# Hybrid decoder step on one core: eight of fourteen input-projection panels per layer computed by seven block products on token halves

## What is computed

```
def mixing_block(x, st, l, P, lb, pos0):
    ...
    proj = jnp.einsum('btd,de->bte', x, P['w_in'][l]).astype(jnp.float32)
    ...
    (xa, ga, qb, kb, vb, ob, ib, fb, qc, kc, vc, gc, qd, fd, id_, gd) = jnp.split(proj, cuts, axis=-1)
    ...
    ya, h1, buf1 = rglru_group(xa, ga, ...)
    yb, c1, n1, m1 = mlstm_group(qb, kb, vb, ob, ib, fb, ...)
    yc, sr1 = retention_group(qc, kc, vc, gc, ...)
    yd, sh1 = hgrn2_group(qd, fd, id_, gd, ...)
    mixed = jnp.concatenate([ya, yb, yc, yd], axis=-1).astype(x.dtype)
```

## Time and profile before

| | |
|---|---|
| time, median of 3 runs | 1056.05 us (1053.13 to 1056.63) |
| the profiled execution's own time | 1044.64 us |
| its span | 1042.8 us |
| input projection and mixers, layer one | about 8 to 180.4 us |
| output projection and normalization, layer one | 180.4 to 217 us |
| dense feed-forward | 217 to 455 us |
| layer two's mixers | the same chain, 447 us later |
| experts and end | 675 to 1042.8 us |

### The profile page before, as it was taken

The page is one execution under the profiler, slowest core; times in us unless marked ns, Lnnn a source line. Parts: engine busy times, 40 slices in busy tenths (PEclk is TensorE's granted clock), DMA queues, the critical chain, the costliest instruction groups (busy, mean ns, idle before and its releaser), DMA issues.

```text
span 1042.8 us, 22726 instructions
## 1 busy us (share of the span) xinstructions
PE 1023.0 (98%) x10341; PEld 740.8 (71%) x10341; DVE 434.4 (42%) x853; ACT 181.8 (17%) x393; POOL 94.3 (9%) x102
## 2 busy tenths in 40 slices
PE   9999999999999999999999999999999999999995
PEld 6787776899999999987877768744545545455552
DVE  5654725555656664148447352621101012010225
ACT  1322223041111100043232231500000000000011
POOL 2000123700000000000011210041000020000010
PEclk9999999999999999999999999999999999999998
DMA  9452238504454235104521429699999999999963
GB/s 334 151 202 82 69 118 301 220 1 162 162 192 162 82 126 228 67 19 143 203 79 44 145 88 367 252 325 357 422 407 409 416 402 408 425 421 424 424 262 113
DMA packets 36548, 240.17 MB, mean 230 GB/s; under 512 B 4768, under 2 KB 8096, under 8 KB 16736
## 3 DMA queue, kind: packets, MB, share of 16 engines
q1 hardware_dynamic: 26896, 216.40, 53.0%
q0 software_dynamic: 6416, 19.52, 5.4%
q10 hardware_dynamic: 3136, 2.75, 0.8%
HBM read 228.60 MB, written 13.07 MB: 232 GB/s over the span
## 4 chain that ended last, share of the span: by engine, by line
PE 93%; DVE 4%; ACT 1%; DMA 1%; issue 1%; SPq 0%; DVEq 0%
PE ps L669 72%; PE ps L1169 14%; PE ps L1274 5%; PE ps L672 1%; DMA up_slots<-in_w_in 1%; DVE x L1992 1%; DVE overlay L1987 0%; ACT overlay L1598 0%; DVE overlay L2123 0%; DVE up_slots L2094 0%; DVE mix_or_moe L2121 0%; DVE overlay L2122 0%; ACT L1598 0%; ACT up_slots L1598 0%; DVE tables L2660 0%
## 5 line engine op out<-in xcount | busy, mean ns | idle before, releaser
L669 PE MATMUL ps<-up_slots,mix_or_moe 128*32 128x352 f32 (+2 forms) x3248 | 245.3, 451 | 0.0
L669 PE MATMUL ps<-x,up_slots 128*128 128x288 f32 (+2 forms) x944 | 233.2, 399 | 0.8 <-DMA up_slots<-in_w_in 0.8
L669 PEld LDWEIGHTS ps<-x,up_slots 128*128 128x128 f32 x944 | 168.9, 190 | 50.8 <-issue 8.3
L669 PEld LDWEIGHTS ps<-up_slots,mix_or_moe 128*32 128x32 f32 (+2 forms) x3248 | 106.6, 111 | 130.5 <-issue 128.8
L669 PE MATMUL ps<-overlay,tables 128*32 128x256 f32 (+5 forms) x2020 | 125.6, 375 | 0.3 <-DVE overlay L1981 0.2
L669 PEld LDWEIGHTS ps<-overlay,tables 128*32 128x32 f32 (+2 forms) x2020 | 76.6, 114 | 46.9 <-issue 5.3
L1169 PE MATMUL ps<-overlay,up_slots 128*128 128x144 f32 x704 | 91.2, 286 | 1.2 <-DVE overlay L2479 1.2
L1169 PEld LDWEIGHTS ps<-overlay,up_slots 128*128 128x128 f32 x704 | 88.2, 190 | 1.4 <-issue 1.4
L669 PE MATMUL ps<-overlay,up_slots 128*128 128x128 f32 (+3 forms) x560 | 86.0, 314 | 1.0 <-ACT overlay L1598 1.0
L2699 DVE TENSOR_TENSOR mix_or_moe<-mix_or_moe,ps 128x352 f32<-128x352 f32 x24 | 11.2, 517 | 178.3 <-PE ps L669 178.3
L669 PEld LDWEIGHTS ps<-overlay,up_slots 128*128 128x128 f32 x560 | 78.2, 191 | 8.6 <-ACT overlay L1598 1.9
(11 more groups left out here) (329 smaller groups left out, 901.2 us busy)
## 6 DMA issues: line engine op xcount, KB each, us to landing
up_slots<-in_moe_w SPq DMA_DIRECT2D x64, 1408.0 KB, 21.0
overlay<-in_moe_w SPq DMA_DIRECT2D x21, 1536.0 KB, 22.5
up_slots<-in_ffn_w SPq DMA_DIRECT2D x30, 1024.0 KB, 6.9
up_slots<-in_w_in SPq DMA_DIRECT2D x27, 1024.0 KB, 4.9
up_slots<-in_w_out SPq DMA_DIRECT2D x8, 1024.0 KB, 9.3
overlay<-in_moe_w SPq DMA_DIRECT2D x7, 1024.0 KB, 22.4
mix_or_moe<-in_states POOLq DMA_DIRECT2D x6, 512.0 KB, 10.5
out_sample_states<-mix_or_moe POOLq DMA_DIRECT2D x6, 512.0 KB, 6.0
```

Of the source, the lines that this page charges most:

```text
L669: return pe.matmul(o, lhsT, rhs, start=start, stop=stop)
```

## The change

Panels 5 to 12 of each layer (VB, KC, QC, ID, VC, GA, GD, GC) are computed by block products. A panel's weights W are four blocks (two halves of the 1024 input channels by its two tiles of outputs), X is four blocks (two halves of the channels by two halves of 144 tokens). Seven products of one weight block or sum of blocks with one X block or sum of blocks take the place of eight; each is four matmuls of 128x128 on 144 tokens. For these panels:

- DVE makes four sums of X once per layer (`token_sums`, 576 elements each), four sums of weights per panel (`panel_sums`, 512 each), and from the products the two output tiles (`panel_outputs`, five operations of 144 and one of 288).
- PE computes the products in three groups of 2, 3 and 2, each group side by side in one PSUM bank, the banks alternating.
- ACT copies each group to SBUF (288, 432 and 288 elements), and before that waits until DVE has used up the same group of the panel before.
- SP loads a panel's blocks once PE has done all products of the panel two before; the output projection's first three weight panels are loaded at the end of the stage and no longer in its middle, the fourth as before after the mLSTM's sample states.
- A tile of such a panel counts as ready when DVE's `panel_outputs` has ended (before: when ACT's copy had).
- On ACT the square and deviation of the retention's norm stand earlier in the order. On the host the weights of these panels are stored block by block.

```
+SEVEN = range(5, 13)
+SEVEN_GROUPS = ((0, 2), (2, 5), (5, 7))
...
+                def token_sums():
...
+                    v.wait_ge(S["in_ps"], N_IN * l + 8)
+                    b11, b12, b21, b22 = (X[:, k:k + KH, c] for k in (0, KH) for c in TOKEN_HALVES)
+                    sig(tt(TX[:, 0], b11, b12, SU), S["sx_t"], 4 * l + 1)
+                    sig(tt(TX[:, 1], b22, TX[:, 0], AD), S["sx_t"], 4 * l + 2)
+                    tt(TX[:, 2], b12, b22, SU).then_inc(S["sx_t"], 1)
+                    tt(TX[:, 3], TX[:, 1], b21, SU).then_inc(S["sx_t"], 1)
...
+                def panel_sums(q, steps=(0, 1, 2, 3)):
+                    w11, w12, w22, w21, s2, s4, s1 = BLOCKS[q % 2]
+                    if 0 in steps:
+                        v.wait_ge(S[f"sx_in_{q % 2}"], loaded["seven", l, q])
+                        tt(s1, w21, w22, AD).then_inc(S["sx_w"], 1)
+                        v.wait_ge(*seven_sum(l, q, 0))
+                    if 1 in steps:
+                        tt(s2, s1, w11, AD).then_inc(S["sx_w"], 1)
+                    if 2 in steps:
+                        tt(w21, w21, w11, AD).then_inc(S["sx_w"], 1)
+                    if 3 in steps:
+                        v.wait_ge(*seven_sum(l, q, 1))
+                        tt(s4, s2, w12, AD).then_inc(S["sx_w"], 1)
...
+                def first_outputs(q):
...
+                    v.wait_ge(*seven_group("sx_ac", l, q, 1))
+                    tt(proj[:, tile, 0:TH], p1, p2, AD)
+                    sig(tt(p6, p6, p1, SU), *seven_out(l, q, 0))
...
+                def last_outputs(q):
...
+                    v.wait_ge(*seven_group("sx_ac", l, q, 2))
+                    tt(p3, p3, p5, AD)
+                    link(tt(p7, p7, p6, AD))
+                    tt(proj[:, tile, TH:T], p3, p6, SU)
+                    sig(tt(proj[:, tile + 1].rearrange("p (h t) -> p h t", h=2), p7.unsqueeze(1).to_broadcast([P, 2, TH]),
+                           SEVEN_OUT[1][:, 0:2], SU), *seven_out(l, q, 1))
...
                 merge(6, 2)
                 chunk_ends()
+                panel_sums(4, (0, 1))
                 mlstm_states()
+                panel_sums(4, (2, 3))
                 merge(7, 2)
...
                 mlstm_spread()
+                panel_outputs(4)
                 need("hg_ps", "c0")
...
+                panel_sums(6)
                 head_rstd(RR_ML, SD_ML, "ml_dv")
...
+                def seven(q, g):
+                    act.wait_ge(*seven_group("sx_pe", l, q, g))
+                    if N_SEVEN * l + q:
+                        act.wait_ge(*seven_out(l, q - 1, min(g, 1)))
...
+                    f(SEVEN_OUT[g], PS[:, (3 * q + g) % 2, 0:n * TH].rearrange("p (n t) -> p n t", n=n), ACT.Copy
+                      ).then_inc(S["sx_ac"], 1)
```

More of the change, by code:

```diff
@@ L209, in mark, with dense, seven_group, seven_sum @@
             return S[name], len(STEPS[name]) * l + STEPS[name].index(step) + 1
+        def dense(i):
+            return i if i // 2 < SEVEN.start else i - 2 * N_SEVEN
+        def seven_group(name, l, q, g):
+            return S[name], 3 * (N_SEVEN * l + q) + g + 1
+        def seven_sum(l, q, i):
+            return S["sx_w"], 4 * (N_SEVEN * l + q) + i + 1
+        def seven_out(l, q, i):
+            return S["sx_dv"], 2 * (N_SEVEN * l + q) + i + 1
         def ev(tile, l):
-            return S["in_ev"], N_IN * l + 2 * ORDER.index(tile - tile % 2) + tile % 2 + 1
+            panel = ORDER.index(tile - tile % 2)
+            if panel in SEVEN:
+                return seven_out(l, panel - SEVEN.start, 1)
+            return S["in_ev"], N_IN * l + dense(2 * panel + tile % 2) + 1
         def ffn(name, step, n):
@@ L342, in decoder_kernel @@
         WD = [cut(UPF, 2048 * s[0], 2 * KD, 256) for s in DOWN_SLOTS]
+        TX = cut(UPF, 3584, 4, KH, TH)
+        BLOCKS = [[cut(UPF, at + 512 * j, KH, P) for j in range(7)] for at in SEVEN_AT]
+        SEVEN_OUT = [cut(UPF, at, n, TH) for at, n in ((9472, 2), (9760, 3), (6 * 2048 + 9530, 2))]
         def panels(name):
@@ L433, in _, with seven_in @@
                     sp.wait_ge(S["up_ps"], 11)
-                for i, tile in enumerate(ORDER):
+                def seven_in(q):
+                    b = q % 2
+                    loaded["seven", l, q] = loaded.get(("n seven", b), 0) + 16
+                    loaded["n seven", b] = loaded["seven", l, q]
+                    sp.dma_start(UPF[:, SEVEN_AT[b]:SEVEN_AT[b] + 2048], w_in[l][SEVEN.start + q]).then_inc(S[f"sx_in_{b}"], 16)
+                for i in range(SEVEN.start):
                     if i >= 2:
@@ L1714, in mix @@
                 level(6)
-                tile(14)
+                seven(2, 0)
                 need("lru_dv", "decay")
@@ L2820, in _arrays @@
     w = a["w_in"]
-    arrays["w_in"] = _panels(w, [128 * tile + (8 if tile >= QC else 0) for tile in ORDER])
+    panels = _panels(w, [128 * tile + (8 if tile >= QC else 0) for tile in ORDER])
+    blocks = panels[:, SEVEN.start:SEVEN.stop].reshape(DEPTH, N_SEVEN, P, 2, KH, 2, P)
+    order = [blocks[:, :, :, half, :, out] for out, half in ((0, 0), (0, 1), (1, 1), (1, 0))]
+    panels[:, SEVEN.start:SEVEN.stop] = np.stack(order, 3).reshape(DEPTH, N_SEVEN, P, -1)
+    arrays["w_in"] = panels
     gates = np.zeros((DEPTH, P, KT, HR), np.float32)
```

199 lines of the change are left out of this document (136 added, 63 removed).

## The result

The changed kernel takes **1064.17 us** (median of 5 runs, 1062.3 to 1066.14) against 1053.13 us for the kernel before (5 runs, 1052.06 to 1056.63): ratio **1.0094, 95% interval 1.007 to 1.0118**. It is slower by some 11 us. I had forecast 1054.9 us, 1046 to 1062, with 0.33 for slower: the time is 2 us outside the range and on the other side of no change. (The forecast stood on a median of 1056.05 us for the kernel before; as a ratio it is 0.9989.)

What follows compares the result with a forecast made beforehand. PE, busy for 98% of the span, was taken to bound the kernel. Per layer, -7.7 us saved plus waits of 1.0, 1.3 and 4.8 gave -0.6, -1.2 in all: 1056.05 to 1054.9 us, range 1046 to 1062.

Steps and rivals of the forecast that it cites:

- 0.33 for slower: Chance of a slower kernel: POOL met twice (0.20), DVE or weights late (0.11), narrow matmuls at their mean cost (0.02).
- PE's saving: Eight changed panels a layer, 28 narrow matmuls for 16 wide: 7.7 us a layer, 15.4 us in all.
- DVE's work: New token sums, weight sums and outputs on DVE: 40 us a layer, some 80 us busy time in all.
- Place 1: Sample states of the mLSTM: PE waits 1.0 us a layer for DVE's states.
- Place 2: The panel VC, behind the retention's scores: PE waits 1.3 us a layer for DVE's outputs of VC.
- Place 3: The mLSTM's head scale: PE waits 4.8 us a layer for DVE's reciprocal, delayed by POOL's third product.
- the instruction named: At the mLSTM's head scale, one weight sum of the seventh changed panel lasts 3 us or more beside POOL.
- POOL's second product: Rival: it starts before DVE's scaled sample queries and holds them, +1.9 us a layer, 1059.9 us; chance 0.20.
- the sum: Per layer PE's saving of 7.7 us less waits of 1.0, 1.3 and 4.8: -0.6 us, -1.2 in all.
- the output projection's second panel: Its weights, issued when the last tile ends, cost PE 0, with bounds of 0 to 1.5 us a layer.
- kind: Prediction is wrong in kind if PE waits for transfers, or for ACT, by more than a microsecond a layer.
- the first one I had named: Sign over the whole kernel: PE's busy time falls by about 15 us, its idle time grows by about 14.

Runs made afterwards that it cites:

- r13: Kernel before with the matmuls of tiles 10 to 25 split into two token halves of 144, nothing left out: ratio 1.0001.
- r10: Kernel before with the fourth of eight matmuls left out of each wide tile 10 to 25, outputs incomplete: ratio 0.9865.
- r7: Changed kernel with the reciprocal ahead of the seventh panel's sums, some fifth- and sixth-panel sums later, clearing later, two feed-forward loads earlier: ratio 1.0092.
- r2: Changed kernel with nine filler matmuls of 288 columns, result unused, ahead of PE's wait for the mLSTM's reciprocal: ratio 1.0052.
- r11: Kernel before with the mLSTM's reciprocal computed four times over, giving PE a wait there: ratio 1.018.
- r3: Changed kernel with POOL's eight clearing transfers of the expert tokens moved behind its feed-forward weight sums: ratio 1.0064.
- r4: The changed kernel again, as it is, against the kernel before on one chip: ratio 1.0103.
- r6: Changed kernel with every weight sum of the changed panels working on one column of 128, so the sums are not computed: ratio 0.9947.
- r9: Changed kernel with c1's copy and reciprocal before the seventh panel's sums, POOL's second and third products later, r7's fifth- and sixth-panel sums, r3's clearing: ratio 0.9885.
- r1: Changed kernel with POOL's third product of each layer waiting until DVE's reciprocal for the mLSTM is done: ratio 0.999.
- r12: As r10, one of eight steps left out of tiles 10 to 25, but each matmul of 288 as two of 144: ratio 0.9867.
- r0: The kernel before again, no edit, run for its profile: ratio 1.0003.
- r5: Changed kernel with DVE taking the mLSTM's reciprocal ahead of the seventh changed panel's weight sums: ratio 1.0105.
- r8: Changed kernel with both r1's edit and r3's edit: ratio 0.9932.

## Why the prediction was wrong

**What held.** PE's saving: 0.245 us a narrow matmul, shown alone by r13 (1.0001), and 15.4 us by count; r10, which leaves out 15.6 us of wide matmuls, is 14 faster with 2.0 us of waits of its own. DVE's work: 80 forecast, 80.4 found. Place 1: 1.0 forecast, 0.96 found. Place 2: 1.3 and 0.92. Place 3: 4.8 and 4.40, by the instruction named. POOL's product there began within DVE's third weight sum and lasted 3.90 instead of 3.62 us, so DVE held it up by a little, too, as the prediction allowed. POOL's second product was not met, as the sum assumed, but that is luck: my own numbers put POOL (119.95) ahead of the queries (120.0), and it came out the other way by 0.15 us. r7 shows the price of the other side.

**What failed** is the step called the sum, in the sentence that behind place 3 "PE waits for nothing new by my count", and in what the sum has no term for. An idle microsecond of PE was priced at one microsecond.

1. **The granted clock behind a wait** was left at 0. It is 10.0 us in the profiled execution, found by its windows, shown by r2 (no idle time, no half clock behind it) and r11 (the wait alone brings it).
2. **Layer one's norm** was left at 0. POOL's weight sums for the feed-forward are late, and the fold of squares meets them. 4.25 us where the same fold had no wait before, and 0.57 for the output projection's second panel, for which I took 0 with bounds of 0 to 1.5. r3 shows the cause: with the clearing's transfers out of the weights' way the sums end 4.4 us earlier, the wait is 0.7 and the weights' 0.57 is gone. I had counted POOL's three products and not its eight sums, and the late issue of three loads but not of the two behind them in SP's list.

The sum again, measured: saving -15.4; waits at the three places 2 x (0.96 + 0.92 + 4.40) = +12.6; layer one's norm and weights +4.6; clock +10.0; together +11.8. The medians say +11.0 and, on r4's chip, +12.4. Without the two terms that I left out it is -2.8, where the forecast was -1.2. The clock's term is that of one execution, at 0.986; the median clock of the five is 0.983, so most lost more.

I wrote that the "kind" would be wrong if PE waited for transfers by over a microsecond a layer. It didn't (0.57). The sign that failed is the first one I had named: PE's busy time was to fall by about 15 us and fell by 1.1, or 4.9 without the experts, because part of the work ran at half clock.

**What stays open.** Why the clock sometimes falls with little or no idle time ahead: at 148 us in r6, 592 us in r9, 102 us in r1 and r12, 562 us in r11. Executions of the kernel before seem to do it too: 9 of 29 beside r0 to r3 have a mean clock of 0.991, against 0.994 to 0.996 for most others, though no profile of such a one was kept. r11 has only wide matmuls in the projection, so the fall does not need narrow ones. One thing the traces share: each of the 16 falls between 90 and 620 us with no wait of PE over 0.5 us in the 8 us ahead of it begins during the products of 32 partitions by 512 (r6's row above), or up to 0.7 us behind them. That alone does not bring a fall, for in the profiles of the kernel before PE passes the same products at a whole clock in both layers; no run changed them. How often it happens in a given version was not settled: r6 had a lower mean clock in most executions, r9 in one of six. Nor was it tried to undo one of r9's edits at a time, so the share of each is known only for r1's and r3's.

## What to carry to other kernels

When PE is the busiest engine, price a wait of it by what its clock does behind it, too: here 10 us of waiting cost about 20. When work moves to a second engine, the question is not whether it fits as a load (it did, at 79%) but what stands behind it in that engine's list, and what a third engine's operation holds up (here POOL's, 3.4 us a layer); moving the late item (r5, r7) only brings the next one to light, so follow the list until the first item that nobody awaits, and put the block there (r9). And follow every transfer queued behind one that became later, up to the engines that consume it.

## What the runs showed of the hardware

- Behind a wait of 4.4 to 5.0 us PE ran at half its clock for 7 to 10 us, in both layers of the changed kernel and of r11. The Trainium skill (TensorE: Matmul & The Clock Gate, HAM oscillation — how this bites in real kernels) tells of a kernel in which each wait for a transfer makes the next stretch start at half rate. The traces agree for these waits, here for DVE. In the prediction I had used the Trainium skill's text on TensorE for the spacing of matmuls only. r6's fall at 149.5 us stands behind no such wait. Filling the wait with matmuls whose result nobody reads kept the clock at 1.00 and made the kernel 0.5% faster than leaving PE idle (r2, 1.0052, against 1.0103).
- Behind r1's waits of 0.92 and 0.96 us in layer one it fell too (0.50 from 140 to 146 us), but not behind the same two in layer two, and it fell in that execution at 102 us with no wait at all. The same holds for r8, where it fell at 138.6 us. Whether a short wait costs clock is open. Each of the 19 waits of 2.55 to 4.97 us between 90 and 620 us, over all profiles, has a fall that begins within it or up to 1.3 us behind it.
- The mean clock orders executions of one kernel: 0.001 is 1 us (r6, 0.993 to 0.982 for 1042.75 to 1053.83 us).
- A matmul of 144 fp32 columns costs half of one of 288 when issued in a row (0.245 and 0.489 us), and splitting 128 of them per layer gave a ratio of 1.0001 (r13).
- A DVE sum of two SBUF operands that started behind POOL's product ended only after it, at each size met: 64 columns took 3.54 us (0.22 alone, r7), 144 took 3.05 (0.29, r9), 512 took 4.12 (0.69, the changed kernel). It ended 0.1 to 0.6 us behind POOL's product each time.
